# Gate and up of the dense feed-forward from chunk 1 on: weights stationary, tokens moving

## The chip, the cores and the metric

One core of one Trainium2 chip runs the whole program. The metric is the device time of one execution in microseconds (us); three runs are shown for the kernel before, and one execution was profiled.

## The reference, cut to what matters

Two stacks of two layers work on one sequence of S = 256 tokens of width D = 1024, in float32. Five feed-forwards among them are dense: one in the first stack's first layer, and two in each layer of the second stack. (The first stack's second layer has a mixture of eight experts instead.)

```python
def swiglu(x, wg, wu, wd):
    return (jax.nn.silu(x @ wg) * (x @ wu)) @ wd
...
def swiglu_2(x, w_gu, w_down):
    gate, up = jnp.split(x @ w_gu, 2, axis=-1)
    return (jax.nn.silu(gate) * up) @ w_down
...
        y = swiglu_2(rmsnorm(h, ffn1_pre_g[l]), ffn1_w_gu[l], ffn1_w_down[l])
        h = h + 0.5 * rmsnorm(y, ffn1_post_g[l])
```

The hidden width is 2816. In the second stack the input is normalised per token, and the result once more.

## The kernel before, in words

**Arithmetic.** Every float32 operand is split into a high part in the matmul's format and a low rest (`uT_hi`, `uT_lo` for the tokens, `hi_a`, `lo_a` for the gate/up weights, `hi_b` or `x_hi` and `lo_b` for the down weights, `hT_hi`, `hT_lo` for the hidden values). A product is three matmuls: high by high, low by high, high by low (`split3`, L660 to L662).

**Chunks.** A feed-forward goes over the hidden width in 11 chunks of 256 columns (`N_FCH`, `FCH`). For a chunk, `gate_up` (TensorE) multiplies the two token tiles of 128 (stationary: `uT`) by 512 moving columns, 256 of gate and 256 of up: 2 tiles x 8 slices of D x 3 products = 48 matmuls of 512 columns, into one PSUM bank per tile (`pp[:, 0]`, `pp[:, 1]`). ACT takes the silu of a tile's gate (`silu`, L1648), DVE multiplies it by the up half (`hidden`, L2286 or L2289), and the hidden values stand in `rows` with tokens on the partitions. The down product needs them the other way round: `turn` (L900) is four 128x128 transposes on TensorE into a bank of `tp`; ACT copies its high part (`hi_hidden`, L1656) and DVE the low one (`turned`, L2300). `down` is then 2 x 2 x 2 x 3 = 24 matmuls of 512 columns into `acc`.

**Order.** `ffn_walk` writes each engine's order: TensorE does `gate_up` of chunk c+1, then `down` of chunk c, then `turn` of chunk c+1. The turn of chunk 0 stands in the middle of `gate_up` of chunk 1, the turn of chunk 10 inside the down product of chunk 9. `gate_up` of a chunk waits on `s_ppv`, that is until DVE has made the chunk before's hidden values and so freed its banks, and on `s_alo` for its weights. ACT's and DVE's orders are fixed as well; in a chunk they hold, beside the steps above, the splitting of the weights two chunks ahead (L1642 and L2276, two halves each) and of the down weights (L1665 and L2313). On DVE a chunk's order is hidden of both tiles, first half of `lo_a`, `hT_lo`, `lo_b`, second half of `lo_a`.

**The per-token factor.** In the second stack `uT` is not yet normalised per token; ACT and DVE multiply by `pre_rstd` where a token is a partition (`scaled=True`: the silu's scale, and the scalar of L2286). POOL makes it in `pre_norm`, and the final normalisation's factor in `post_norm`.

Of the kernel before, what the change touches and what calls it, by code (L numbers as in the profile page):

```python
# [23 lines left out]
F32 = mybir.dt.float32  # L24
F32R = mybir.dt.float32r
# [7 lines left out]
P = 128  # L33
# [147 lines left out]
def program(nc, a, out):  # L181
    with ExitStack() as ctx:
# [29 lines left out]
        uT_hi = sb("uT_hi", [P, KD, S], F32R)  # L212
        uT_lo = sb("uT_lo", [P, KD, S], F32R)
# [44 lines left out]
        nlam = stat[:, 128:129]  # L258
        nsink = stat[:, 136:144]
# [14 lines left out]
        hi_c = x_hi[:, :, :].rearrange("p t d -> p (t d)")  # L274

# [54 lines left out]
        s_ppv = sem("s_ppv")  # L330
        s_acc = [sem("s_acc0"), sem("s_acc1")]
# [321 lines left out]
        def _(pe):  # L653
# [186 lines left out]
            def ffn(experts, sparse=False, ahead=False):  # L840

                a0, b0, g0, lo0, ppv0 = n["a"], n["b"], n["g"], n["lo"], n["ppv"]
                tiles = 1 if sparse else TT

# [24 lines left out]
                def gate_up(c, e, j):  # L869
# [6 lines left out]
                    if c.rest == 0:  # L876
                        wait_pp()
                    else:
                        pe.wait_ge(s_ppv, c.half * 4 + (2 * c.rest - opening + ppv0))
                    if sparse and isinstance(j, int) and j == 0:  # L880
                        pe.wait_ge(s_glo, e.index + 1)
                    wh = hi_a[:, slot, :].rearrange("p (g k n) -> p g k n", g=2, k=KD)
                    wl = lo_a[:, slot, :].rearrange("p (g k n) -> p g k n", g=2, k=KD)
                    for tt in range(tiles):
                        if opening and tt == 1:
                            turn(Chunk(c.half, c.rest - 1))
# [6 lines left out]
                def turn(c):  # L893
# [3 lines left out]
                    for kk in range(2):  # L897
                        for tt in range(tiles):
                            at = (kk * tiles + tt) * P
                            mm = nc.tensor.transpose(tp[:, bank, at:at + P],  # L900
# [34 lines left out]
                def side_b(c, e, j):  # L935
                    if not sparse and isinstance(j, int) and j == 0 and is_first(e):
                        pe.wait_ge(s_accfree, n["acc"])
                    if experts == 1 and isinstance(j, int) and j == N_FCH - 2:
                        enter(c)
                        part(c, 0, 0, e, j)  # L940
                        turn(c.next())
                        part(c, 0, 1, e, j)
                        part(c, 1, 0, e, j)
                        return
# [6 lines left out]
                    down(c, e, j).then_inc(s_bused, 1)  # L951
                    turn(c.next())
# [14 lines left out]
                def tail(c, e, j):  # L967
# [16 lines left out]
                    for tt in range(TT):  # L984
                        if experts == 1 and tt == 1:
                            part(Chunk(c.half, c.rest - 1), 1, 1, e, j - 1).then_inc(s_bused, 1)
                        for h in range(2):
                            part(c, 0, tt, e, j, (h,))
                            if ahead and tt == 1 and h == 1:
                                bank_free[0] = bank_free[1] = (s_tlo, lo0 + experts * N_FCH)  # L990
                                turn_ahead(g0 + experts * N_FCH, lo0 + experts * N_FCH)
# [6 lines left out]
                n["g"] += k  # L998
# [6 lines left out]
                pp_free[:] = [(s_ppv, n["ppv"] - 1), (s_ppv, n["ppv"])]  # L1005
# [123 lines left out]
            def mixer():  # L1129

                n["unit"] = 0
                fill_free[:] = pp_free
# [390 lines left out]
            for l in range(N_LAYERS):  # L1523
# [3 lines left out]
                ffn(1, ahead=True)  # L1527
# [3 lines left out]
                ffn(1, ahead=l + 1 < N_LAYERS)  # L1531
# [3 lines left out]
        def _(act):  # L1535
# [90 lines left out]
            def ffn(experts, final=False, sparse=False, scaled=False):  # L1626
                a1, b0, g0, pp0, bu0 = n["a"], n["b"], n["g"], n["pp"], n["bu"]
                tiles = 1 if sparse else TT
                last = experts * N_FCH - 1
# [14 lines left out]

                def silu(c, which=range(tiles)):
                    for tt in which:
                        act.wait_ge(s_pp, c.half * 4 + (2 * c.rest + tt + 1 + TT - tiles + pp0))
# [4 lines left out]
                def hi_hidden(c):  # L1652
                    slot = (b0 - 1 + c.rest) % 2
                    act.wait_ge(s_tps, c.at(g0 + 1))
                    ks = slice(slot, slot + 1) if sparse else slice(2 * slot, 2 * slot + 2)
                    nc.scalar.activation(hT_hi[:, ks, :].rearrange("p k s -> p (k s)"),  # L1656
                                         tp[:, (g0 + c.rest) % 2, 0:tiles * S], ACT.Copy).then_inc(s_thi, 1)
# [29 lines left out]
                def body(c, e, j):  # L1687
# [19 lines left out]
                    else:  # L1707
                        silu(c)
                        hi_next(c, 0)
# [24 lines left out]
                n["g"] += k  # L1734
                n["pp"] += 2 * k

# [388 lines left out]
        def _(dve):  # L2125
# [132 lines left out]
            def ffn(experts, final=False, sparse=False, scaled=False):  # L2258
                a1, b0, g0, hi0, ppa0, half0 = n["a"], n["b"], n["g"], n["thi"], n["ppa"], n["half"]
                bu0 = n["bu"] + 2  # L2260
                tiles = 1 if sparse else TT
                left = []

# [16 lines left out]

                def hidden(c, e, which=range(tiles)):
                    for tt in which:
                        dve.wait_ge(s_ppa, c.half * 4 + (2 * c.rest + tt + 1 + TT - tiles + ppa0))
                        o, s, u = rows[:, tt, FCH:2 * FCH], rows[:, tt, 0:FCH], pp[:, tt, FCH:2 * FCH]
                        if scaled:
                            ins = nc.vector.scalar_tensor_tensor(out=o, in0=s, scalar=pre_rstd[:, tt:tt + 1], in1=u,  # L2286
# [1118 lines left out]
```

## Time and profile before

| | |
|---|---|
| median of 3 runs | 2534.42 us (2533.99 to 2536.29) |
| span of the profiled execution | 2530.3 us |
| mean granted TensorE clock | 0.997 |
| PE busy | 98% of the span |
| weight loads (PEld) | 81% |
| DVE, ACT, POOL busy | 70%, 55%, 10% |

The span goes from the first to the last instruction. The profiled execution's own time is not listed; the runs shown lie 3.7 to 6.0 us above its span. Matmuls are pipelined: the duration of one (389 ns for 512 columns) is longer than the distance between two starts, and it is the distance between starts that adds up.

### The profile page before, as it was taken

How to read it: one execution, taken by the hardware profiler on the slowest of the kernel's cores; microseconds unless marked ns; L12 is line 12 of the kernel's file. 1: busy time of each engine (PE TensorE's matmuls, PEld its weight loads, DVE VectorE, ACT ScalarE, POOL GpSimd, SP SyncE). 2: the span in 40 equal slices, each digit the busy share in tenths (PEclk: the TensorE clock that was granted, in tenths of full speed). 3: DMA queues.
4: the chain of work that ended last, by engine and by line, in shares of the span. 5: the costliest groups of instructions: out<-in, count | busy, mean ns of one | idle time of the engine just before them, and what ended most of it. 6: DMA issues, size and time to landing. Idle time of an engine off the chain costs nothing.

```text
span 2530.3 us, 32402 instructions
## 1 busy us (share of the span) xinstructions
PE 2481.9 (98%) x11877; PEld 2036.9 (81%) x11877; DVE 1770.7 (70%) x1750; ACT 1395.4 (55%) x1524; POOL 248.4 (10%) x317
## 2 busy tenths in 40 slices
PE   9999999999999999999999999999999999999998
PEld 7778877878888888887788888878888888887887
DVE  5755557789989989999755667785555556778554
ACT  5543444677777777777644555454444445554533
POOL 3000021000000000000141103010004210300000
PEclk9999999999999999999999999999999999999999
DMA  7354444699999999999785343355548644435551
GB/s 274 142 224 175 174 137 172 259 360 366 368 364 358 371 361 363 368 368 353 264 263 212 135 190 142 135 208 208 190 160 253 220 153 172 166 142 199 196 187 67
DMA packets 89577, 595.83 MB, mean 235 GB/s; under 512 B 11616, under 2 KB 11760, under 8 KB 22016
## 3 DMA queue, kind: packets, MB, share of 16 engines
q1 hardware_dynamic: 77760, 558.99, 58.2%
q0 software_dynamic: 11712, 35.43, 5.1%
q8 instruction: 67, 1.10, 0.2%
q14 instruction: 38, 0.31, 0.0%
HBM read 588.09 MB, written 6.29 MB: 235 GB/s over the span
## 4 chain that ended last, share of the span: by engine, by line
PE 80%; DVE 9%; ACT 4%; issue 3%; DMA 3%; POOL 1%; SPq 0%; DVEq 0%; ACTq 0%; POOLq 0%
PE pp L660 17%; PE pp L662 17%; PE pp L661 17%; PE acc L660 7%; PE acc L662 7%; PE acc L661 7%; DVE lo_a L2797 2%; PE tp L900 2%; DMA raw_a<-in_moe_gu 1%; ACT hi_a L1581 1%; DVE lo_a L2185 1%; PE tp L672 1%; PE acc L1040 1%; PE tp L1089 1%; DVE lo_b L2313 1%
## 5 line engine op out<-in xcount | busy, mean ns | idle before, releaser
L660 PE MATMUL pp<-hi_a,uT_hi 128*128 128x512 f32 (+1 forms) x2140 | 852.5, 398 | 10.1 <-DVE uT_lo L2660 2.7
L662 PE MATMUL pp<-hi_a,uT_lo 128*128 128x512 f32 (+1 forms) x2140 | 832.4, 389 | 0.0
L661 PE MATMUL pp<-lo_a,uT_hi 128*128 128x512 f32 (+1 forms) x2140 | 830.4, 388 | 0.0
L2276 DVE TENSOR_TENSOR lo_a<-raw_a,hi_a 128x2048 fp32r<-128x2048 f32 x282 | 649.7, 2304 | 125.6 <-ACT hi_a L1642 124.7
L1642 ACT ACTIVATE hi_a<-raw_a 128x2048 fp32r<-128x2048 f32 x282 | 537.9, 1909 | 23.7 <-DMA raw_a<-in_moe_gu 23.2
L660 PEld LDWEIGHTS pp<-hi_a,uT_hi 128*128 128x128 f32 x2140 | 402.1, 188 | 92.0 <-issue 9.9
L662 PEld LDWEIGHTS pp<-hi_a,uT_lo 128*128 128x128 f32 x2140 | 401.7, 188 | 85.7
L661 PEld LDWEIGHTS pp<-lo_a,uT_hi 128*128 128x128 f32 x2140 | 402.8, 188 | 76.4
L661 PE MATMUL acc<-lo_b,hT_hi 128*128 128x512 f32 x792 | 308.2, 389 | 0.0
L2313 DVE TENSOR_TENSOR lo_b<-raw_b,hi_b 128x2048 fp32r<-128x2048 f32 x115 | 263.4, 2290 | 44.9 <-ACT hi_b L1665 44.0
L660 PE MATMUL acc<-hi_b,hT_hi 128*128 128x512 f32 x572 | 223.8, 391 | 2.8 <-DVE lo_b L2313 2.8
L662 PE MATMUL acc<-hi_b,hT_lo 128*128 128x512 f32 x572 | 223.0, 390 | 0.0
L1665 ACT ACTIVATE hi_b<-raw_b 128x2048 fp32r<-128x2048 f32 x115 | 220.0, 1913 | 4.0 <-DMA raw_b<-in_moe_wd 3.8
L1581 ACT ACTIVATE hi_a<-raw_a 128x2048 fp32r<-128x2048 f32 (+1 forms) x104 | 190.5, 1875 | 21.6 <-PE pp L662 13.9
L1656 ACT ACTIVATE hT_hi<-tp 128x256 fp32r<-128x256 f32 (+1 forms) x143 | 66.6, 466 | 243.2 <-PE tp L900 242.8
L661 PEld LDWEIGHTS acc<-lo_b,hT_hi 128*128 128x128 f32 x792 | 148.7, 188 | 30.3
L2797 DVE TENSOR_TENSOR lo_a<-raw_a,hi_a 128x2048 fp32r<-128x2048 f32 (+1 forms) x64 | 143.0, 2269 | 41.4 <-ACT hi_a L1581 39.8
L1648 ACT ACTIVATE rows<-pp,stat 128x256 f32<-128x256 f32 x88 | 41.8, 475 | 233.6 <-PE pp L662 230.7
L2300 DVE TENSOR_TENSOR hT_lo<-tp,hT_hi 128x256 fp32r<-128x256 f32 (+1 forms) x143 | 74.7, 523 | 111.3 <-ACT hT_hi L1656 111.3
L1648 ACT ACTIVATE rows<-pp 128x256 f32<-128x256 f32 x110 | 42.3, 385 | 186.6 <-PE pp L662 183.3
L2286 DVE SCALAR_TENSOR_TENSOR rows<-rows,stat,pp 128x256 f32<-128x256 f32 x88 | 41.6, 476 | 133.2 <-ACT rows L1648 133.2
L660 PEld LDWEIGHTS acc<-hi_b,hT_hi 128*128 128x128 f32 x572 | 107.4, 188 | 28.3 <-issue 3.9
(303 smaller groups left out, 2744.0 us busy)
## 6 DMA issues: line engine op xcount, KB each, us to landing
raw_a<-in_moe_gu SPq DMA_DIRECT2D x176, 1024.0 KB, 6.6
raw_a<-in_ffn_w_gu SPq DMA_DIRECT2D x88, 1024.0 KB, 6.7
raw_b<-in_moe_wd SPq DMA_DIRECT2D x87, 1024.0 KB, 8.5
raw_a<-in_w_in SPq DMA_DIRECT2D x70, 1024.0 KB, 6.8
raw_b<-in_ffn_w_down SPq DMA_DIRECT2D x44, 1024.0 KB, 4.9
raw_a<-in_ffn_gu SPq DMA_DIRECT2D x22, 1024.0 KB, 6.6
raw_a<-in_w_out SPq DMA_DIRECT2D x16, 1024.0 KB, 5.9
raw_a<-in_w_branch SPq DMA_DIRECT2D x12, 1024.0 KB, 6.0
```

The source lines that it names most:

```text
L660: nc.tensor.matmul(out_ap, l_hi, r_hi, start=start, stop=False, skip_group_check=True)
L661: nc.tensor.matmul(out_ap, l_hi, r_lo, start=False, stop=False, skip_group_check=True)
L662: return nc.tensor.matmul(out_ap, l_lo, r_hi, start=False, stop=stop, skip_group_check=True)
L1581: nc.scalar.activation(hi_a[:, slot, cs], raw_a[:, slot, cs], ACT.Copy) \
L1642: nc.scalar.activation(hi_a[:, slot, cs], raw_a[:, slot, cs], ACT.Copy) \
L1648: nc.scalar.activation(rows[:, tt, 0:FCH], pp[:, tt, 0:FCH], ACT.Silu, scale=pre_rstd[:, tt:tt + 1] if scaled else 1.0) \
L1656: nc.scalar.activation(hT_hi[:, ks, :].rearrange("p k s -> p (k s)"), tp[:, (g0 + c.rest) % 2, 0:tiles * S], ACT.Copy).then_inc(s_thi, 1)
L1665: nc.scalar.activation(dst[:, :], raw_b[:, slot, :] if src is None else src, ACT.Copy) \
L2276: ins = nc.vector.tensor_tensor(lo_a[:, slot, cs], raw_a[:, slot, cs], hi_a[:, slot, cs].bitcast(F32), ALU.subtract)
L2300: nc.vector.tensor_tensor(hT_lo[:, ks, :].rearrange("p k s -> p (k s)"), tp[:, (g0 + c.rest) % 2, 0:tiles * S], hT_hi[:, ks, :].rearrange( ...
L2313: nc.vector.tensor_tensor(lo_b[:, slot, :], src, hb[:, :].bitcast(F32), ALU.subtract).then_inc(s_blo, 1)
L2797: ins = nc.vector.tensor_tensor(lo_a[:, slot, cs], raw_a[:, slot, cs], hi_a[:, slot, cs].bitcast(F32), ALU.subtract)
```

## The change

From chunk 1 on, the weights are the stationary operand and all 256 tokens move. A chunk has two blocks of 128 hidden columns; for each, gate and up get a bank of their own: `tp[:, 0]`, `tp[:, 1]` for block 0 and `pp[:, 1]`, `pp[:, 0]` for block 1 (`block_bank`). Into a bank go, for each of the 8 slices of D, one matmul of 512 columns (high weights by high and low tokens side by side, which is why `uT` is now one tensor) and one of 256 (low weights by high tokens). That is 2 x 2 x 8 x 2 = 64 matmuls, 32 of each width. The bank then holds two halves that must still be added. The result has hidden columns on the partitions, as `down` needs it, so there is no turn for these chunks.

ACT copies the half with the low tokens to `rows` (`low_part`), DVE adds it to the other half (`block_sums`), for gate and for up; silu runs from `rows`, and `hT_hi` and `hT_lo` are made from `rows`. Chunk 0 stays as it was, with its turn, now into `pp[:, 0]`.

In the second stack a token is now a column, so DVE multiplies the gate's sum by a full tile `by_token` (one more operation per block); two transposes on TensorE (`turn_factors`) and an ACT copy (`factors`) make it at the start of chunk 1. The up half is left without the factor, and `post_norm` makes up for it with a scaled epsilon (`post_eps`).

```diff
+                def turn_factors():
...
+                    pe.wait_ge(s_pre, n["pre"])
+                    for tt in range(TT):
+                        mm = nc.tensor.transpose(pp[:, 0, tt * P:(tt + 1) * P],
+                                                 pre_rstd[:, tt:tt + 1].to_broadcast([P, P]), ident[:, :])
+                    mm.then_inc(s_tps, 1)
...
+                    for block in range(2):
+                        if opening and block == 1:
+                            if scaled:
+                                pe.wait_ge(s_bytoken, n["bytoken"])
+                            turn(Chunk(0, 0))
+                        ws = slice(block * P, (block + 1) * P)
+                        for g in range(2):
+                            if opening and block and g:
+                                pe.wait_ge(s_tlo, lo0 + 1)
+                            bank = block_bank(block, g)
+                            for k in range(KD):
+                                nc.tensor.matmul(bank.rearrange("p (c s) -> p c s", c=2), wh[:, g, k, ws], uT[:, :, k, :],
+                                                 start=(k == 0), stop=False, skip_group_check=True)
+                                mm = nc.tensor.matmul(bank[:, 0:S], wl[:, g, k, ws], uT_hi[:, k, :], start=False,
+                                                      stop=(k == KD - 1), skip_group_check=True)
+                            mm.then_inc((s_gate, s_pp)[g], 1)
...
+                    if dense and not (isinstance(j, int) and j == 0):
+                        if opening and scaled:
+                            turn_factors()
+                        gate_up_blocks(slot, opening)
+                        return
...
                     if experts == 1 and isinstance(j, int) and j == N_FCH - 2:
                         enter(c)
-                        part(c, 0, 0, e, j)
-                        turn(c.next())
-                        part(c, 0, 1, e, j)
-                        part(c, 1, 0, e, j)
+                        for kk, tt in ((0, 0), (0, 1), (1, 0)):
+                            part(c, kk, tt, e, j)
                         return
...
                     down(c, e, j).then_inc(s_bused, 1)
+                    if dense:
+                        return
                     turn(c.next())
...
                     for tt in which:
+                        if dense and not is_opening(c):
+                            low_part(c, tt, 0)
+                            act.wait_ge(s_gsum, c.half * 4 + (2 * c.rest + tt - 1 + gate0))
+                            nc.scalar.activation(rows[:, tt, 0:FCH], rows[:, tt, 0:FCH], ACT.Silu).then_inc(s_ppa, 1)
+                            low_part(c, tt, 1)
+                            continue
...
+                    if dense and not is_opening(c):
+                        act.wait_ge(s_ppv, c.half * 4 + (2 * c.rest + 2 + pp0))
+                        nc.scalar.activation(hT_hi[:, 2 * slot:2 * slot + 2, :], rows[:, :, FCH:2 * FCH], ACT.Copy) \
+                          .then_inc(s_thi, 1)
+                        return
...
+                    dve.wait_ge(s_low, c.half * 8 + (4 * c.rest + 2 * block - 3 + low0))
+                    ins = nc.vector.tensor_tensor(gate, block_bank(block, 0)[:, 0:S], low_gate, ALU.add)
+                    if scaled:
+                        ins.then_inc(s_graw, 1)
...
+                        ins = nc.vector.tensor_tensor(gate, gate, by_token, ALU.mult)
+                    ins.then_inc(s_gsum, 1)
+                    dve.wait_ge(s_low, c.half * 8 + (4 * c.rest + 2 * block - 2 + low0))
+                    nc.vector.tensor_tensor(low_up, block_bank(block, 1)[:, 0:S], low_up, ALU.add).then_inc(s_upsum, 1)
+                    dve.wait_ge(s_upsum, c.half * 4 + (2 * c.rest + block - 1 + low0 // 2))
+                    dve.wait_ge(s_ppa, c.half * 4 + (2 * c.rest + block + 1 + ppa0))
+                    nc.vector.tensor_tensor(rows[:, block, FCH:2 * FCH], gate, low_up, ALU.mult).then_inc(s_ppv, 1)
```

On TensorE, where a down product ends and the next `gate_up` begins (second stack, first feed-forward, chunk 1 to chunk 2), there stood before:

```order
L661 MATMUL acc<-lo_b,hT_hi 128x512
L662 MATMUL acc<-hi_b,hT_lo 128x512
L900 MATMUL tp<-ident,rows 128x128 [waits s_tlo,s_ppv]
L900 MATMUL tp<-ident,rows 128x128 x3
L660 MATMUL pp<-hi_a,uT_hi 128x512 [waits s_ppv,s_alo]
L661 MATMUL pp<-lo_a,uT_hi 128x512
L662 MATMUL pp<-hi_a,uT_lo 128x512
```

And now (lines are those of the changed kernel):

```order
L675 MATMUL acc<-lo_b,hT_hi 128x512
L676 MATMUL acc<-x_hi,hT_lo 128x512
L889 MATMUL tp<-uT,hi_a 128x512 [waits s_ppv,s_alo]
L891 MATMUL tp<-uT,lo_a 128x256
L889 MATMUL tp<-uT,hi_a 128x512
L891 MATMUL tp<-uT,lo_a 128x256
```

The four transposes are gone; the wait on `s_ppv` now stands at the first matmul of `gate_up` alone, and matmuls of two widths alternate.

On DVE, from the hidden values of chunk 0 to those of chunk 1 in the same feed-forward, there stood before:

```order
L2286 SCALAR_TENSOR_TENSOR rows<-rows,stat,pp 128x256 [waits s_ppa,s_pre]
L2286 SCALAR_TENSOR_TENSOR rows<-rows,stat,pp 128x256 [waits s_ppa]
L2276 TENSOR_TENSOR lo_a<-raw_a,hi_a 128x2048 [waits s_ahalf]
L2300 TENSOR_TENSOR hT_lo<-tp,hT_hi 128x512 [waits s_thi]
L2313 TENSOR_TENSOR lo_b<-raw_b,x_hi 128x2048 [waits s_bhi]
L2276 TENSOR_TENSOR lo_a<-raw_a,hi_a 128x2048 [waits s_ahi]
L2286 SCALAR_TENSOR_TENSOR rows<-rows,stat,pp 128x256 [waits s_ppa] x2
```

And now:

```order
L2376 TENSOR_TENSOR lo_a<-raw_a,hi_a 128x2048 [waits s_ahi]
L2386 TENSOR_TENSOR rows<-tp,rows 128x256 [waits s_low]
L2392 TENSOR_TENSOR rows<-rows,qkT 128x256 [waits s_graw,s_bytoken]
L2395 TENSOR_TENSOR rows<-tp,rows 128x256 [waits s_low]
L2398 TENSOR_TENSOR rows<-rows 128x256 [waits s_ppa,s_upsum]
L2386 TENSOR_TENSOR rows<-pp,rows 128x256 [waits s_low]
L2392 TENSOR_TENSOR rows<-rows,qkT 128x256 [waits s_graw]
L2395 TENSOR_TENSOR rows<-pp,rows 128x256 [waits s_low]
L2398 TENSOR_TENSOR rows<-rows 128x256 [waits s_ppa,s_upsum]
```

Behind the same second half of `lo_a`, two operations have become eight, with waits on ACT between them (`s_low` for the copies, `s_ppa` for the silu). `qkT` is where `by_token` lies; in the first stack L2392 is missing.

## Rows read from the trace of the kernel before

**Rows 1.** The page's first part: busy us, share of the span, instructions

```profile
PE 2481.9 (98%) x11877; PEld 2036.9 (81%) x11877; DVE 1770.7 (70%) x1750; ACT 1395.4 (55%) x1524; POOL 248.4 (10%) x317
```

**Rows 2.** Windows: one stretch in each dense feed-forward; columns in its first row

```profile
core 0: us, PE busy (x) PEld busy (x) DVE busy (x) ACT busy (x) POOL busy (x), PEclk, DMA share, GB/s
147.00:316.00 169.00, 168.88 (x766) 139.47 (x765) 88.99 (x71) 73.22 (x65) 0.79 (x2) 1.00 0.51 188
1264.00:1432.00 168.00, 168.00 (x763) 139.00 (x762) 93.10 (x66) 74.98 (x67) 39.75 (x50) 1.00 0.64 219
...
sum 839.00, PE 838.88 PEld 693.83 DVE 443.73 ACT 366.05 POOL 80.61; mean PE 167.78 PEld 138.77 DVE 88.75 ACT 73.21 POOL 16.12
```

**Rows 3.** Timeline of PE around one turn: start, duration, line, tile, count

```profile
1292.20 0.39 PE L662 MATMUL acc<-hi_b,hT_lo 128*128 128x512 f32 x1
1292.43 0.60 PE L900 MATMUL tp<-ident,rows 128*128 128x128 f32 x4
1292.78 0.48 PE L660 MATMUL pp<-hi_a,uT_hi 128*128 128x512 f32 x1
1293.10 0.40 PE L661 MATMUL pp<-lo_a,uT_hi 128*128 128x512 f32 x1
...
1294.03 0.39 PE L662 MATMUL pp<-hi_a,uT_lo 128*128 128x512 f32 x1
```

**Rows 4.** Timeline of PE: first turn, and the turns before and after

```profile
1264.26 0.60 PE L900 MATMUL tp<-ident,rows 128*128 128x128 f32 x4
...
1275.63 0.60 PE L900 MATMUL tp<-ident,rows 128*128 128x128 f32 x4
...
1309.24 0.60 PE L900 MATMUL tp<-ident,rows 128*128 128x128 f32 x4
```

**Rows 5.** Timeline of PE far from any turn

```profile
1300.17 0.39 PE L662 MATMUL pp<-hi_a,uT_lo 128*128 128x512 f32 x1
1300.40 0.39 PE L660 MATMUL pp<-hi_a,uT_hi 128*128 128x512 f32 x1
...
1303.57 0.39 PE L662 MATMUL pp<-hi_a,uT_lo 128*128 128x512 f32 x1
```

**Rows 6.** Timeline of PE and PEld in the mixer's 256-wide projection

```profile
1475.50 0.28 PE L662 MATMUL pp<-hi_a,uT_lo 128*128 128x256 f32 x1
1475.62 0.28 PE L660 MATMUL pp<-hi_a,uT_hi 128*128 128x256 f32 x1
...
1478.02 0.28 PE L662 MATMUL pp<-hi_a,uT_lo 128*128 128x256 f32 x1
...
1475.39 0.19 PEld L662 LDWEIGHTS pp<-hi_a,uT_lo 128*128 128x128 f32 x1
1475.51 0.19 PEld L660 LDWEIGHTS pp<-hi_a,uT_hi 128*128 128x128 f32 x1
```

**Rows 7.** Groups of instructions by line and form: count, busy us, mean ns

```profile
L662 PEld LDWEIGHTS pp<-hi_a,uT_lo 128*128 128x128 f32 x2140 | 401.7, 188 | 85.7
L2289 DVE TENSOR_TENSOR rows<-rows,pp 128x256 f32<-128x256 f32 x110 | 45.4, 413 | 37.0 <-ACT rows L1648 37.0
L2768 DVE TENSOR_TENSOR t<-mixb,rope 128x256 f32<-128x256 f32 x8 | 3.0, 418 | 0.1
L1648 ACT ACTIVATE rows<-pp 128x256 f32<-128x256 f32 x110 | 42.3, 385 | 186.6 <-PE pp L662 183.3 <-PE pp L865 3.2
L1656 ACT ACTIVATE hT_hi<-tp 128x512 fp32r<-128x512 f32 x55 | 32.9, 599 | 192.6 <-PE tp L900 192.6
```

**Rows 8.** Timeline of ACT and DVE from the first turn on (idle before, releaser)

```profile
1264.90 0.60 ACT L1656 ACTIVATE hT_hi<-tp 128x512 fp32r<-128x512 f32 x1 [4.34 <-PE tp L900]
1265.39 1.91 ACT L1665 ACTIVATE x_hi<-raw_b 128x2048 fp32r<-128x2048 f32 x1
1267.20 1.91 ACT L1642 ACTIVATE hi_a<-raw_a 128x2048 fp32r<-128x2048 f32 x1
1269.00 0.46 ACT L1648 ACTIVATE rows<-pp,stat 128x256 f32<-128x256 f32 x1
...
1265.53 0.69 DVE L2300 TENSOR_TENSOR hT_lo<-tp,hT_hi 128x512 fp32r<-128x512 f32 x1 [2.65 <-ACT hT_hi L1656]
1267.34 2.29 DVE L2313 TENSOR_TENSOR lo_b<-raw_b,x_hi 128x2048 fp32r<-128x2048 f32 x1 [1.12 <-ACT x_hi L1665]
1269.54 2.28 DVE L2276 TENSOR_TENSOR lo_a<-raw_a,hi_a 128x2048 fp32r<-128x2048 f32 x1
1271.75 0.86 DVE L2286 SCALAR_TENSOR_TENSOR rows<-rows,stat,pp 128x256 f32<-128x256 f32 x2
```

More of the change, by code:

```diff
@@ L274, in program, with block_bank @@
         hi_c = x_hi[:, :, :].rearrange("p t d -> p (t d)")
+        by_token = qkT[:, 0, 0:S]
+        def block_bank(block, g):
+            return (pp[:, 1 - g, :] if block else tp[:, g, :])
         def centred(tt):
@@ L1004, in ffn @@
                     bank_free[0] = bank_free[1] = (s_tlo, n["lo"])
-                pp_free[:] = [(s_ppv, n["ppv"] - 1), (s_ppv, n["ppv"])]
+                pp_free[:] = [(s_ppv, n["ppv"] - (not dense)), (s_ppv, n["ppv"])]
                 n["acc"] += 1
@@ L1628, in ffn @@
                 tiles = 1 if sparse else TT
+                dense, gate0 = experts == 1, n["gate"]
+                turns = 1 + scaled if dense else experts * N_FCH
                 last = experts * N_FCH - 1
@@ L1708, in body @@
                         silu(c)
+                        if scaled and is_opening(c):
+                            factors()
                         hi_next(c, 0)
@@ L2259, in ffn, with is_opening @@
                 a1, b0, g0, hi0, ppa0, half0 = n["a"], n["b"], n["g"], n["thi"], n["ppa"], n["half"]
+                low0, graw0 = n["low"], n["graw"]
                 bu0 = n["bu"] + 2
                 tiles = 1 if sparse else TT
+                dense = experts == 1
+                turns = 1 + scaled if dense else experts * N_FCH
                 left = []
+                if scaled:
+                    n["bytoken"] += 1
+                def is_opening(c):
+                    return isinstance(c.half, int) and c.at(0) == 0
                 def rest():
@@ L2298, in turned @@
                     dve.wait_ge(s_thi, c.at(hi0 + 1))
+                    if dense and not is_opening(c):
+                        ks = slice(2 * slot, 2 * slot + 2)
+                        nc.vector.tensor_tensor(hT_lo[:, ks, :], rows[:, :, FCH:2 * FCH], hT_hi[:, ks, :].bitcast(F32),
+                                                ALU.subtract).then_inc(s_tlo, 1)
+                        return
                     ks = slice(slot, slot + 1) if sparse else slice(2 * slot, 2 * slot + 2)
                     nc.vector.tensor_tensor(hT_lo[:, ks, :].rearrange("p k s -> p (k s)"),
-                                            tp[:, (g0 + c.rest) % 2, 0:tiles * S],
+                                            (pp[:, 0, :] if dense else tp[:, (g0 + c.rest) % 2, :])[:, 0:tiles * S],
                                             hT_hi[:, ks, :].rearrange("p k s -> p (k s)").bitcast(F32),
@@ L2377, in ffn @@
                 n["bu"] += k - 1
-                n["g"] += k
+                n["g"] += turns
+                if dense:
+                    n["low"] += 4 * (k - 1)
+                if scaled:
+                    n["graw"] += 2 * (k - 1)
                 n["thi"] += k
```

87 lines of the change are left out of this document (62 added, 25 removed).

## The prediction

> **What bounds the kernel now.** The page first: PE is busy for 98% of the span, weight loads for 81%, DVE for 70% and ACT for 55% [rows 1]. That is an average, so the stretches in which the change acts are read next: in one window in each dense feed-forward PE is busy 838.88 of 839.00 us, at a granted clock of 1.00 (the 2.4 GHz level), while DVE has 443.73 and ACT 366.05 us of work in them [rows 2]. In these stretches no other engine ends a wait, and the time is the sum of what TensorE issues. That sum is read from starts, not from durations. Far from a turn, 512-wide matmuls start every (1303.57 - 1300.17) / 15 = 0.2267 us [rows 5]. A chunk has 48 + 24 = 72 of them, 16.32 us. From turn to turn it takes (1309.24 - 1275.63) / 2 = 16.805 us [rows 4]. The difference, 0.485 us, is the price of a turn, and the timeline shows where it lies: the four transposes start at 1292.43, just where the next matmul would have, and the sixth matmul of `gate_up` starts at 1294.03, not at 1292.43 + 5 x 0.2267 = 1293.56 [rows 3].
>
> **What the change removes.** Of 11 turns in a feed-forward the one of chunk 0 stays. 10 x 5 = 50 turns go: 50 x 0.485 = -24.3 us.
>
> **What it adds on TensorE.** The columns stay the same (32 x 768 = 48 x 512), but 48 matmuls become 64, and each has its own start. The nearest row for a 256-wide one is the mixer's 256-wide projection: they start every (1478.02 - 1475.50) / 21 = 0.120 us [rows 6]. A chunk's `gate_up` is then 32 x (0.2267 + 0.120) = 11.09 us in place of 48 x 0.2267 = 10.88: +0.213, in 50 chunks +10.7 us. No row shows the two widths in turn. The bound below is half a wide one, 0.113 (nothing added); the bound above is the slow rival below. I take the sum of the two rows, because in either stretch the distance is the columns' time plus about 13 ns, so nothing but the columns sets it.
>
> What speaks against 256-wide matmuls is the weight load: one shows 188 ns [rows 7], longer than 120. But in that stretch the loads start 0.12 us apart and overlap [rows 6]. The Trainium skill ("TensorE: Matmul & The Clock Gate", Back-to-back issue gap) gives a warm distance of N/2.4 + 2.5 ns, 215.8 and 109.2; by it the added cost would be 0.042 us a chunk and the forecast 8.6 us lower, but the trace differs by 11 ns at either width, and the sum goes by the trace.
>
> In the four scaled feed-forwards `turn_factors` adds two transposes: by the turn's price less two starts of 0.11 us (within a turn, (1292.78 - 1292.43) / 4 = 0.09 to 0.485 / 4 = 0.12 each [rows 3]) 0.27 us each, in all +1.1 us. What they wait for (`s_pre`, the first tile's hidden values) is what the first silu and this `gate_up` waited for before.
>
> **What it adds on ACT and DVE, and what hides it.** Per block: ACT two copies and a silu of 256 columns, 0.385 us each by the silu's row; DVE two sums from PSUM, 0.413, and one or two products in SBUF, 0.418 [rows 7]. A scaled chunk has some 3.3 us of such DVE work in place of 0.95: ten chunks add some 24 us to some 90 in a window of 168 [rows 2]. As work it is covered; what counts is a wait that comes too late.
>
> In steady state that is `s_ppv`, before the next `gate_up`. Behind the last up matmul stand: ACT copy 0.39, DVE sum 0.41, product 0.42, with hops of about 0.04 (the copy ends at 1265.50, DVE starts at 1265.53 [rows 8]): some 1.35 us. `down` of the chunk before covers 24 x 0.2267 = 5.44. Cost nothing; without that cover it would be the 1.35.
>
> At the end, `down` of chunk 10 waits for `s_tlo`: those 1.35, then the ACT copy 0.60 and DVE's rest 0.69 [rows 7, 8], some 2.7 us, behind 18 matmuls of chunk 9, 4.08 us. Nothing again, with 1.4 us to spare. Before, the turn sat between.
>
> At the opening it is different. From the first turn ACT does `hT_hi`, the down weights' high part and half of `hi_a`, up to 1269.0; DVE follows with `hT_lo`, `lo_b` and half of `lo_a`, and comes to chunk 1's hidden values at 1271.75, 7.49 us behind the turn's start [rows 8]. Both tiles then took 0.86. TensorE wanted them at 1275.63, 11.37 behind [rows 4]; now, with 16 pairs in place of 24 wide matmuls in between (+0.11), at 11.48. So 4.0 us are there. In them DVE has two blocks to do, and each is a chain: sum 0.41, times `by_token` 0.42, silu and copy on ACT 0.68 (the second starts about 0.09 before the first ends), sum 0.41, product 0.42, four hops 0.16: 2.5 us. The second block's data are long there, but DVE and ACT take the blocks in order, so two blocks are 5.0 us. TensorE stands for 1.0 us before `gate_up` of chunk 2. In the unscaled feed-forward a block is 2.04 and two are 4.1: 0.1. In all 4 x 1.0 + 0.1 = +4.1 us. Bounds: nothing, if operations overlap more; 2 us each, if a hop costs 0.15. Late next is chunk 1's own splitting and so chunk 2's hidden values; there DVE has another 11 + 5.4 us, and nothing more is lost.
>
> The larger `ss` work on POOL is one operation on two columns behind `s_pre`, beside TensorE's matmuls; no DMA is added or moved.
>
> **Sum.** -24.3 + 10.7 + 1.1 + 4.1 = -8.4 us on a span of 2530.3. The median lies 4.1 above that span, by what no row shows and the change doesn't touch: 2534.4 - 8.4 = 2526.0 us.
>
> **Rivals.**
> - *Weight loads bind, and it becomes slower.* With 88 loads of 188 ns a chunk has 16.5 us of them in about 16.5 us. If a narrow matmul between wide ones can't hide the next load, a pair costs two loads, 376 ns, not 347: 32 x 50 x 0.029 = +47 us, 2573 us. It decides from a pair of 352 ns on, since 1600 x 5.3 ns eat the 8.4 us. The overlapping loads speak against it [rows 6]; for it, that no row has the two widths mixed. The Trainium skill ("Perfetto Trace Analysis", Identifying the Most-Contended Engine) would judge TensorE by the busy share of loads, which by its rule would leave no room here; the 256-wide stretch, where loads fill more than the time, does not bear that out as a bound.
> - *A wait in every chunk.* If the ping-pong between ACT and DVE ends later than 5.44 us behind the last matmul, each chunk loses; 0.17 us a chunk make it no faster, 0.5 make it 2542 us. The chain has 4 us to spare.
> - *No stall at the opening.* The chains overlap better than I add them: 2526.0 - 4.1 = 2521.9 us.
> - *Twice the stall at the opening, or one at the end too.* Some 1 us more at 4 or 5 places: 2530 to 2531 us, the same as far as can be told.
> - *The change does nothing*, because the turn's time was a wait's in disguise: against it, PE's busy 838.88 of 839.
>
> **How the numbers follow.** About 0.2%, 5 us, is what a measurement of this kernel can tell from no change. The forecast as summed (2522.5 to 2529) has 0.55, no stall at the opening 0.16: faster 0.71. More stall, or nothing gained, 0.14: same. Loads that bind 0.09, waits in every chunk or at other places 0.06: slower 0.15. The range goes from a stall of nothing with a slightly dearer turn, 2520.5, to 2532.5, where a doubled stall meets pairs a few ns dearer; it leaves the slow cases and a part of the case without change outside.
>
> **What the profile afterwards would show.** `gate_up` at 11.09 us and a chunk at 16.53 from one first matmul to the next, with starts 0.227 and 0.120 us apart in turn; any pair above 0.35 makes the second term wrong. One turn in each dense feed-forward. Idle time of PE before the first matmul of `gate_up` of chunk 2, put down to DVE's product at L2398, about 1 us in four feed-forwards and near nothing in the first; idle there in other chunks makes the covers wrong. No idle before the down product of chunk 10. DVE some 100 us busier in all.

## The result, and the profile after

The changed kernel takes 2546.1 us in the median, the kernel before, timed beside it, 2537.8: a ratio of 1.0031 (1.0017 to 1.0046), slower by 8 us where the prediction said 8 us faster. Timed again on another occasion the ratio was 1.0034 (1.0020 to 1.0048). The profiled execution has a span of 2544.3 us, 14.0 above the one that the sum was made against. Three executions that were disturbed as a whole (4103 us of the changed kernel, 11290 and 2603 us of two experiments) are left out of everything.

The page's first part of the changed kernel, to be held against [rows 1]:

```profile
PE 2485.5 (98%) x12485; PEld 2059.2 (81%) x12485; DVE 1885.7 (74%) x2030; ACT 1461.9 (57%) x1728; POOL 252.4 (10%) x321
```

DVE is 115 us busier, some 100 were forecast, and ACT 66. TensorE has 608 matmuls more and is still busy for 98%: what made the kernel slower must again be read from starts, in two places.

**The chunk.** The timeline of PE in the middle of a `gate_up` of the changed kernel (start, duration, line, tile):

```profile
1355.94 0.40 PE L889 MATMUL tp<-uT,hi_a 128*128 128x512 f32 x1
1356.17 0.28 PE L891 MATMUL tp<-uT,lo_a 128*128 128x256 f32 x1
1356.29 0.40 PE L889 MATMUL tp<-uT,hi_a 128*128 128x512 f32 x1
1356.53 0.28 PE L891 MATMUL tp<-uT,lo_a 128*128 128x256 f32 x1
...
1360.18 0.40 PE L889 MATMUL pp<-uT,hi_a 128*128 128x512 f32 x1
```

Twelve pairs take 4.24 us, 0.3535 each, not 0.3467. The narrow matmul costs 0.117, no more than among its own kind; it is the wide one that takes some 0.236 where it took 0.2267 among wide ones [rows 5]. And the starts of two down products six chunks apart, with the `gate_up` that follows the first, in the same view:

```profile
1315.45 0.40 PE L674 MATMUL acc<-x_hi,hT_hi 128*128 128x512 f32 x1
...
1320.96 0.39 PE L889 MATMUL tp<-uT,hi_a 128*128 128x512 f32 x1
...
1416.21 0.40 PE L674 MATMUL acc<-x_hi,hT_hi 128*128 128x512 f32 x1
```

A chunk takes 100.76 / 6 = 16.793 us. Its down product takes 1320.96 - 1315.45 = 5.51 of them, the rest, 11.28, is `gate_up`; forecast were 5.44 and 11.09. Before, a chunk took 16.805 [rows 4]. The turn is gone, and nothing came of it.

**The opening.** The waits of PE over the span (us in all, times, longest), and the starts of the first two down products of the first scaled feed-forward:

```profile
PE tp L889 <- DVE rows L2398: 4.8, 4, 1.8
```

```profile
1278.51 0.40 PE L674 MATMUL acc<-x_hi,hT_hi 128*128 128x512 f32 x1
...
1298.71 0.40 PE L674 MATMUL acc<-hi_b,hT_hi 128*128 128x512 f32 x1
```

Four waits of 1.84, 1.04, 0.94 and 1.04 us before `gate_up` of chunk 2, where they were expected and put down to the product that was named, with 1.0 each forecast. But in the feed-forward with the 1.84 this chunk takes 20.20 us, 3.4 more than the others. The windows there (columns as in [rows 2]) and the timeline show what lies behind the wait:

```profile
1284.00:1286.00 2.00, 0.16 (x2) 0.06 (x1) 1.04 (x3) 1.78 (x3) 0.14 (x1) 1.00 1.13 373
1286.00:1288.00 2.00, 2.00 (x7) 1.77 (x8) 1.26 (x1) 2.00 (x3) 0.00 (x0) 0.58 0.86 242
1288.00:1290.00 2.00, 2.00 (x8) 1.66 (x8) 2.00 (x3) 2.00 (x2) 0.00 (x0) 0.57 1.02 422
1290.00:1292.00 2.00, 2.00 (x13) 1.75 (x12) 2.00 (x2) 1.10 (x2) 1.29 (x3) 1.00 0.55 225
```

```profile
1285.97 0.47 PE L889 MATMUL tp<-uT,hi_a 128*128 128x512 f32 x1 [1.84 <-DVE rows L2398]
...
1286.45 0.63 PE L889 MATMUL tp<-uT,hi_a 128*128 128x512 f32 x1
1286.88 0.41 PE L891 MATMUL tp<-uT,lo_a 128*128 128x256 f32 x1
1287.09 0.63 PE L889 MATMUL tp<-uT,hi_a 128*128 128x512 f32 x1
```

TensorE had stood idle for 1.84 us; then the granted clock is 0.58 and 0.57 in two windows (most of each at 1.2 GHz), a pair takes 0.64 us, and at 1290 the clock is back at 1.00. Nearly half of that chunk's loss is this, not the wait.

**The stages that weren't changed.** Up to the last down product the two profiles differ by 14.0 us. 7.4 of them lie between the end of the first feed-forward and the end of the mixture of experts, and only 6.6 in all the rest: 918.3 us before, 925.7 after. More on that below.

### The profile page after: what moved, and what is told of

Its sections match the earlier page's. It is cut to its first block, busy times and chain, and to the rows that moved or that the text cites. A ratio compares the mean times of both kernels' runs of the same rounds, so it can differ in the third digit from the quotient of the medians.

```text
span 2544.3 us, 34318 instructions
## 1 busy us (share of the span) xinstructions
PE 2485.5 (98%) x12485; PEld 2059.2 (81%) x12485; DVE 1885.7 (74%) x2030; ACT 1461.9 (57%) x1728; POOL 252.4 (10%) x321
## 4 chain that ended last, share of the span: by engine, by line
PE 75%; DVE 10%; DMA 5%; ACT 5%; issue 4%; POOL 1%; SPq 0%; DVEq 0%; ACTq 0%; POOLq 0%
PE pp L674 9%; PE pp L676 9%; PE pp L675 9%; PE tp L889 7%; PE pp L889 7%; PE acc L674 6%; PE acc L676 6%; PE acc L675 6%; PE tp L891 4%; PE pp L891 3%; DMA raw_b<-in_moe_wd 3%; DVE lo_a L2925 2%; DMA raw_a<-in_moe_gu 1%; DVE lo_a L2376 1%; ACT hi_a L1635 1%
## 5 line engine op out<-in xcount | busy, mean ns | idle before, releaser
L674 PE MATMUL pp<-hi_a,uT 128*128 128x512 f32 (+1 forms) x1340 | 536.7, 400 | 6.1 <-ACT rows L2059 2.3
L676 PE MATMUL pp<-hi_a,uT 128*128 128x512 f32 (+1 forms) x1340 | 521.3, 389 | 0.0
L675 PE MATMUL pp<-lo_a,uT 128*128 128x512 f32 (+1 forms) x1340 | 519.7, 388 | 0.0
L674 PEld LDWEIGHTS pp<-hi_a,uT 128*128 128x128 f32 x1340 | 252.4, 188 | 56.5 <-issue 8.2
L676 PEld LDWEIGHTS pp<-hi_a,uT 128*128 128x128 f32 x1340 | 252.0, 188 | 53.8
L889 PE MATMUL tp<-uT,hi_a 128*128 128x512 f32 x800 | 286.3, 400 | 5.5 <-DVE rows L2398 4.8
L675 PEld LDWEIGHTS pp<-lo_a,uT 128*128 128x128 f32 x1340 | 252.8, 189 | 46.7
L889 PE MATMUL pp<-uT,hi_a 128*128 128x512 f32 x800 | 284.8, 399 | 0.0
L2437 DVE TENSOR_TENSOR lo_b<-raw_b,hi_b 128x2048 fp32r<-128x2048 f32 x115 | 263.2, 2289 | 20.5 <-ACT hi_b L1752 20.1
L891 PE MATMUL tp<-uT,lo_a 128*128 128x256 f32 x800 | 225.3, 282 | 0.0
L891 PE MATMUL pp<-uT,lo_a 128*128 128x256 f32 x800 | 224.6, 281 | 0.0
L889 PEld LDWEIGHTS tp<-uT,hi_a 128*128 128x128 f32 x800 | 151.1, 189 | 44.0 <-issue 6.8
L889 PEld LDWEIGHTS pp<-uT,hi_a 128*128 128x128 f32 x800 | 150.3, 188 | 36.9
```

The lines of the kernel that those rows point to most:

```text
L674: nc.tensor.matmul(out_ap, l_hi, r_hi, start=start, stop=False, skip_group_check=True)
L675: nc.tensor.matmul(out_ap, l_hi, r_lo, start=False, stop=False, skip_group_check=True)
L676: return nc.tensor.matmul(out_ap, l_lo, r_hi, start=False, stop=stop, skip_group_check=True)
L889: nc.tensor.matmul(bank.rearrange("p (c s) -> p c s", c=2), wh[:, g, k, ws], uT[:, :, k, :], start=(k == 0), stop=False, skip_group_check= ...
L891: mm = nc.tensor.matmul(bank[:, 0:S], wl[:, g, k, ws], uT_hi[:, k, :], start=False, stop=(k == KD - 1), skip_group_check=True)
L2437: nc.vector.tensor_tensor(lo_b[:, slot, :], src, hb[:, :].bitcast(F32), ALU.subtract).then_inc(s_blo, 1)
```

## The experiments

**The turn alone.** The kernel before, with the transposes of chunks 1 to 10 left out in the dense feed-forwards:

```diff
                 pe.wait_ge(s_tlo, c.at(lo0 - 1))
+                if experts == 1 and c.rest + (0 if isinstance(c.half, int) else 2) > 0:
+                    pe.sem_inc(s_tps, 1)
+                    return
                 for kk in range(2):
```

> The kernel before with the transposes of chunks 1 to 10 left out in its dense feed-forwards (their results are then not those of the reference: the hidden values' turned form is stale); the waits stay. It measures the first term alone: if a turn costs what was read, 0.485 us, a chunk is 16.32 us and the kernel 24 us faster than the kernel before, some 2513. If something else paces a chunk at 16.79, which is what both kernels take, it stays there and nothing is gained.

It took 2509.6 us, ratio 0.9894 (0.9877 to 0.9910): 27 us less, between 23 and 31. Its rows come from a second run:

> The kernel before without the transposes of chunks 1 to 10 once more, for its rows: a chunk of 72 wide matmuls at 16.32 us if the price of a turn is 0.485, between 16.32 and 16.80 if part of the price was the widths' change or a wait.

2510.3 us, and in the timeline the starts of down products six chunks apart:

```profile
1299.94 0.39 PE L660 MATMUL acc<-x_hi,hT_hi 128*128 128x512 f32 x1
...
1397.86 0.39 PE L660 MATMUL acc<-x_hi,hT_hi 128*128 128x512 f32 x1
```

97.92 / 6 = 16.320 us, to the last digit what 72 wide matmuls were said to take. The price of a turn was right, and nothing else paces a chunk at 16.79: that both kernels take nearly the same is chance.

**The pair by itself.** The changed kernel with some 570 matmuls behind its last one, while the other engines run out of work (`wide_rows` moves 512 columns of weights, `wide_blocks` both parts of the tokens as L889 does, `narrow` is as L891):

```diff
...
+            for wide_one in (wide_rows, wide_blocks):
+                for i in range(48):
+                    wide_one(i % KD)
+                for i in range(48):
+                    wide_one(i % KD)
+                    narrow(i % KD)
+                for run in (2, 8):
+                    for i in range(48 // run):
+                        for k in range(run):
+                            wide_one(k)
+                        for k in range(run):
+                            narrow(k)
...
```

> The changed kernel with some 570 matmuls behind its last one, on operands that are left there (no output depends on them), while the other engines finish and then stand idle: 48 wide ones in a row, 48 pairs, runs of two and two and of eight and eight, first with a wide matmul whose moving operand is one piece (weights), then with the two-piece one (high and low part of the tokens), then 64 narrow ones. If the change of width is what costs: wide in a row 227 ns for both kinds, pairs 354 for both, runs of eight some 348 per pair. If the two-piece operand costs: 227 in a row for one kind and 236 for the other. If ACT's and DVE's work beside it costs: pairs at 347 here, where nothing runs beside them. In time some 130 us longer.

The timeline of PE: the one-piece kind in a row and in pairs, then its runs of two, then two starts of runs of eight (a row with x2 or x49 is a group, and begins at its first start), then the two-piece kind:

```profile
2536.50 11.27 PE L1593 MATMUL tp<-hi_a,uT 128*128 128x512 f32 x49
2547.60 0.28 PE L1597 MATMUL pp<-uT,lo_a 128*128 128x256 f32 x1
2547.72 0.40 PE L1593 MATMUL tp<-hi_a,uT 128*128 128x512 f32 x1
...
2562.09 0.28 PE L1597 MATMUL pp<-uT,lo_a 128*128 128x256 f32 x1
...
2565.02 0.63 PE L1593 MATMUL tp<-hi_a,uT 128*128 128x512 f32 x2
2565.49 0.39 PE L1597 MATMUL pp<-uT,lo_a 128*128 128x256 f32 x2
2565.72 0.63 PE L1593 MATMUL tp<-hi_a,uT 128*128 128x512 f32 x2
2566.18 0.40 PE L1597 MATMUL pp<-uT,lo_a 128*128 128x256 f32 x2
2566.41 0.40 PE L1593 MATMUL tp<-hi_a,uT 128*128 128x512 f32 x1
...
2583.82 0.40 PE L1593 MATMUL tp<-hi_a,uT 128*128 128x512 f32 x1
...
2586.61 0.40 PE L1593 MATMUL tp<-hi_a,uT 128*128 128x512 f32 x1
...
2597.79 11.30 PE L1589 MATMUL tp<-uT,hi_a 128*128 128x512 f32 x49
2608.92 0.28 PE L1597 MATMUL pp<-uT,lo_a 128*128 128x256 f32 x1
...
2610.69 0.28 PE L1597 MATMUL pp<-uT,lo_a 128*128 128x256 f32 x1
```

In a row a wide one takes (2547.60 - 2536.50) / 49 = 0.2265, the two-piece kind 0.2271. In pairs it is (2562.09 - 2547.60) / 41 = 0.3534 and (2610.69 - 2608.92) / 5 = 0.354. So it is neither the operand in two pieces nor the work of ACT and DVE, which stood still from 2544 on: it is the alternation. Runs of two bring four wide and four narrow ones to 1.39 us, 0.348 a pair; runs of eight take 2.79 / 8 = 0.349. Neither is the sum of the two rows, 0.3465, but both lie much nearer to it than the pairs in turn.

**The order in the kernel.** First eight and eight within each bank:

```diff
                             for k in range(KD):
                                 nc.tensor.matmul(bank.rearrange("p (c s) -> p c s", c=2), wh[:, g, k, ws], uT[:, :, k, :],
                                                  start=(k == 0), stop=False, skip_group_check=True)
+                            for k in range(KD):
                                 mm = nc.tensor.matmul(bank[:, 0:S], wl[:, g, k, ws], uT_hi[:, k, :], start=False,
```

> Order within a bank changed: the eight 512-wide matmuls first, then the eight 256-wide ones, in place of pairs. If it is the change of width that makes a wide matmul dear (236 ns behind a narrow one in the changed kernel, 227 among its own kind) and only the first one behind a narrow one pays, gate_up is 32 x (0.2281 + 0.120) = 11.14 us in place of 11.32 and the kernel some 9 us faster than the changed one, some 2537. If the slowness dies out over seven to ten matmuls, as the rows behind the turns of the kernel before show it, the wide ones still average some 232 ns, gate_up is some 11.26 and only 3 us come back. If wide matmuls are slow because their moving operand comes in two pieces (high and low part of the tokens), or because ACT and DVE read PSUM beside them, they stay at 236 in a row: gate_up 11.4, no gain.

2535.0 us, ratio 0.9997 (0.9985 to 1.0008) to the kernel before, some 9 us less than the changed kernel has by its ratios, as the first case of the expectation says. In the timeline, down products six chunks apart:

```profile
1314.26 0.40 PE L674 MATMUL acc<-x_hi,hT_hi 128*128 128x512 f32 x1
...
1413.94 0.40 PE L674 MATMUL acc<-x_hi,hT_hi 128*128 128x512 f32 x1
```

A chunk takes 99.68 / 6 = 16.613: 0.18 less, in 50 chunks 9 us, from the order of the same 64 matmuls. Then all 32 wide ones first:

```diff
                         for g in range(2):
                             if opening and block and g:
                                 pe.wait_ge(s_tlo, lo0 + 1)
...
+                            wide_part(block, g)
+                            if opening:
+                                narrow_part(block, g)
+                    if not opening:
+                        for block in range(2):
+                            for g in range(2):
+                                narrow_part(block, g)
```

> From chunk 2 on all 32 wide matmuls of gate_up first, then the 32 narrow ones, bank by bank; chunk 1 stays in pairs. Cost of changing widths: the narrow ones cost 32 x 0.120 = 3.84 us, the wide ones 32 x 0.227 = 7.26 plus some 0.06 for the slow first ones, gate_up 11.16 in place of 11.32 and, with some 0.06 in down behind the narrow ones as now, a chunk of 16.63: 45 x 0.16 = 7 us faster than the changed kernel, some 2539. Rival, two-piece operand or contention: wide ones at 236 in a row, gate_up 11.4, no gain. The gates come ready only in the last 3.8 us of gate_up, so the last hidden values end some 2 us behind it; down covers 5.4, and no new wait is expected.

Chunk 1 (`opening`) has eight wide and eight narrow ones a bank in this code, not the pairs that the expectation names. In the timeline, down products six chunks apart:

```profile
1313.38 0.40 PE L674 MATMUL acc<-x_hi,hT_hi 128*128 128x512 f32 x1
...
1412.70 0.40 PE L674 MATMUL acc<-x_hi,hT_hi 128*128 128x512 f32 x1
```

A chunk takes 99.32 / 6 = 16.553 us, even less than expected and within 0.02 of the prediction's 16.53: kept apart, the two widths cost what it added up. But the kernel takes 2555.7, ratio 1.0077 (1.0057 to 1.0098). The new wait that wasn't expected is there, five times, 14.9 us in all. In the first scaled feed-forward the waits of PE and the timelines of DVE and ACT read:

```profile
PE acc L674 <- DVE hT_lo L2432: 3.2, 1, 3.2
```

```profile
1429.09 0.43 DVE L2410 TENSOR_TENSOR rows<-rows 128x256 f32<-128x256 f32 x1
1430.43 2.29 DVE L2449 TENSOR_TENSOR lo_b<-raw_b,x_hi 128x2048 fp32r<-128x2048 f32 x1 [0.92 <-ACT x_hi L1764]
1432.64 0.42 DVE L2398 TENSOR_TENSOR rows<-pp,rows 128x256 f32<-128x256 f32 x1
...
1435.85 0.69 DVE L2432 TENSOR_TENSOR hT_lo<-rows,hT_hi 128x512 fp32r<-128x512 f32 x1 [0.69 <-ACT hT_hi L1744]
```

In chunk 10 alone the code puts the low part of the down weights (2.29 us on DVE, behind 1.90 on ACT) between the two blocks. With pairs, block 0 is through before; with the gates of all blocks coming at the end, the second block waits for it, and the down product for the second block. The expectation counted two blocks and left that step out.

**The opening.** Chunk 0's turn one bank earlier in `gate_up` of chunk 1:

```diff
                     for block in range(2):
-                        if opening and block == 1:
-                            if scaled:
-                                pe.wait_ge(s_bytoken, n["bytoken"])
-                            turn(Chunk(0, 0))
...
                         for g in range(2):
+                            if opening and not block and g:
+                                if scaled:
+                                    pe.wait_ge(s_bytoken, n["bytoken"])
+                                turn(Chunk(0, 0))
```

> The turn of chunk 0 stands before the first block's up part in chunk 1's gate_up, 2.8 us earlier than between its blocks. If the wait before gate_up of chunk 2 (1.84, 1.04, 0.94 and 1.04 us in the four scaled feed-forwards, some 0.1 in the other) comes from what ACT and DVE do behind that turn, it goes wholly: 4.9 us faster than the changed kernel, some 2541. Rival: chunk 0's hidden values and the copy of the factors are late for the earlier turn, and TensorE waits there, up to 0.5 us each; 3 us come back. Rival: the wait is set by DVE's two blocks alone: no change.

2534.1 us, ratio 0.9994 (0.9984 to 1.0004), by the ratios some 10 us less than the changed kernel. No wait of L889 for L2398 is left, and the first scaled feed-forward's down products of chunks 0 and 1 start, in the timeline:

```profile
1269.24 0.40 PE L674 MATMUL acc<-x_hi,hT_hi 128*128 128x512 f32 x1
...
1286.00 0.40 PE L674 MATMUL acc<-hi_b,hT_hi 128*128 128x512 f32 x1
```

16.76 us apart, in place of 20.20; in the other feed-forwards 16.74 to 16.76 in place of 18.04, 17.94, 17.84 and 16.96. That is 3.4 + 1.3 + 1.2 + 1.1 + 0.2 = 7.2 us for waits of 4.9 us. The other two profiles of the changed kernel, read in the same way, lose 7.0 us for 5.0 us of waits, with a fallen clock, and 5.1 us for 4.6, with the clock at 1.00 throughout. The timed runs show some 3 us more than 7.2; in the profiles the mixture of experts is 3 to 4 us shorter as well, see below.

**Both.** Wide first in chunks 2 to 9, bank by bank in chunks 1 and 10, the turn early:

```diff
-                        gate_up_blocks(slot, opening)
+                        gate_up_blocks(slot, opening, opening or isinstance(j, int) and j == N_FCH - 1)
```

> The changed kernel with the early turn of chunk 0, the wide matmuls first in chunks 2 to 9, and bank by bank (eight wide, eight narrow) in chunks 1 and 10, so that the last chunk's gates don't all come ready at the end. If the costs found so far add up: chunks 2 to 9 at 16.55 us and chunk 10 at 16.61, where the kernel before takes 16.80, no wait at the opening and none before the last down product: 40 x 0.25 + 10 x 0.19 = 12 us faster than the kernel before, some 2524, ratio 0.995. If the gain of the order and that of the early turn overlap or a new wait comes at the end (up to 3 us in each feed-forward): 2530 to 2536.

2528.2 us, ratio 0.9970 (0.9959 to 0.9982): faster than both kernels. In its timeline:

```profile
1305.60 0.40 PE L674 MATMUL acc<-x_hi,hT_hi 128*128 128x512 f32 x1
...
1404.92 0.40 PE L674 MATMUL acc<-x_hi,hT_hi 128*128 128x512 f32 x1
```

99.32 / 6 = 16.553 us a chunk, and neither wait in any of the five. Without the stretch from the first feed-forward's end to the end of the mixture of experts, the time to the last down product is 1594.4 us, 10.6 to 12.9 less than in three profiles of the kernel before; the median shows 7.5 of it.

**The stages that weren't changed.** The changed kernel again, timed, then both kernels side by side on one chip:

> The changed kernel once more, beside the kernel before. The dense feed-forwards' own rows make it some 6.5 us slower (ratio 1.0026); the other 7 us of difference between the two profiles lie in the mixture of experts, whose code is the same. If that stage varies from run to run, the ratio is 1.0015 to 1.0035 and the stage takes some other time in this profile, between 917 and 926 us; if the change slows that stage too, it is 1.004 or more and the stage takes 925 again.

> The kernel before once more, for the stages that the change doesn't touch. So far the mixture of experts took 778 to 782 us in two profiles of kernels with the old dense feed-forward and 784 to 786 in three of the changed one. If the stage only varies from run to run, it falls anywhere from 777 to 788 here; if the change slows it, it is 782 or less again.

> The changed kernel, on the same chip as the two looks at the kernel before. If the mixture of experts only varies from run to run, it takes 777 to 788 us; if the change slows it, 784 or more once more.

> As the other look at the kernel before: 777 to 788 us in the mixture of experts if it only varies, 782 or less if the changed kernel alone is slow there.

From the first matmul that gathers tokens for an expert (L822, in the changed kernel L836) to the last down product of the mixture of experts, the three profiles of the kernel before have 778.3, 778.2 and 781.6 us, the one without turns 782.2; the changed kernel has 784.8, 783.8 and 783.6, and 786.1 with the added matmuls behind it. With eight and eight the stage takes 788.5, and wide first 786.3. ACT's waits for that stage's weights in two profiles from one chip, first `before_b`, then `after_c`:

```profile
ACT hi_a L1642 <- DMA raw_a<-in_moe_gu: 17.9, 22, 2.4
```

```profile
ACT hi_a L1698 <- DMA raw_a<-in_moe_gu: 30.7, 29, 2.8
```

The weights come later there. The other two profiles of the kernel before have 23.2 and 26.0 us of these waits, of the changed kernel 32.0 and 31.3. With the early turn in all five feed-forwards the stage took 780.5 and, with the wide ones first as well ("Both"), 781.8 us, so the turn was moved in the scaled feed-forwards alone (g1, below) and in the unscaled one alone (g2, with `not scaled`):

```diff
-                        if opening and block == 1:
+                        if opening and block == 1 and not (scaled):
...
+                            if opening and not block and g and scaled:
```

> The early turn in the four scaled feed-forwards alone, which all run after the mixture of experts. Dense rows: some 7 us faster than the changed kernel. If the expert stage's 4 us follow from what runs ahead of it, they stay (784 us or more there, 31 us of waits for its gate-up weights), and the kernel is some 2538; if they follow from how the program as a whole lies, or from chance, the stage can take 778 to 782.

> The early turn in the unscaled feed-forward alone, the one that runs ahead of the mixture of experts. Dense rows: 0.2 us faster than the changed kernel. If the expert stage's lateness comes from that feed-forward's opening, the stage takes 780 to 782 us with some 20 us of waits and the kernel is some 4 us faster than the changed one; if not, 784 or more and no change.

> The early turn in all five once more, for the expert stage alone: 780 to 782 us with some 20 us of waits for gate-up weights if that was no chance; 784 or more if it was.

The profiles have 791.7 us (42.5 of waits) in g1, 784.3 (31.8) in g2 and 780.8 (23.4) in the repeat. By these g1 is the worst of all, but its profiled execution is the slowest of its ten (2545.9; they go down to 2533.5), and its median is 2538.0, ratio 1.0012 (0.9999 to 1.0025), by the ratios some 5 us under the changed kernel's where its dense rows ask for 7. g2 has 1.0019 (1.0000 to 1.0038), too wide to tell whether anything was gained. All eight profiles of the new feed-forwards without the early turn in all five lie above 783.5 us in this stage, the other seven profiles at or below 782.2. But up to the end of this stage g2 does the same work in the same order as the kernel with the early turn, and takes 784.3 where that took 780.5 and 780.8, so what runs ahead of the stage doesn't explain it by itself. Single profiles of one kernel differ by 3.4 us in this stage, and by some 4 in the mixer ahead of it (136.4 and 140.0 us in two of the kernel before): the longer one has a granted clock of 0.5 from 442 to 452 us, the other 1.00. Whether the changed kernel is really some 3 us slower there, and by what, stays open.

## Why the prediction was wrong, by its own steps

**What bounds the kernel, and the turn's price.** Right: 0.485 us read, 16.805 - 16.320 measured, 50 x 0.485 = -24.3, and 23 to 31 us in the timed runs.

**The 16 added matmuls.** This is the step that failed: "the sum of the two rows, because in either stretch the distance is the columns' time plus about 13 ns, so nothing but the columns sets it". Both rows were of stretches of one width. In turn a pair takes 0.3535, and `gate_up` 11.28 in place of 10.88, +0.40. The down product behind it takes 5.51 in place of 5.44, a term that the prediction didn't have. Together a chunk pays 16.793 - 16.320 = 0.473 for the added matmuls, not 0.213. In 50 chunks that is +23.7 us in place of +10.7, and nearly the whole gain of the turns. The prediction named the pair's price from which the sign turns, 352 ns, and gave it 9 in 100. The price came, 353.5 ns, but not by that rival's reason: two loads one behind the other would be 376 ns, and in runs of two the same loads cost 348 a pair. The runs show that the mixture costs more than its parts; why it does stays open. The Trainium skill's warm gap of a single matmul ("TensorE: Matmul & The Clock Gate", Back-to-back issue gap) errs on the same side: an estimate by it is 215.8 + 109.2 = 325 ns a pair.

**The factors.** Right, small. Timeline of PE at the third scaled opening:

```profile
1910.40 0.38 PE L869 MATMUL pp<-ident,stat 128*128 128x128 f32 x2
1910.54 0.48 PE L889 MATMUL tp<-uT,hi_a 128*128 128x512 f32 x1
1910.97 0.40 PE L889 MATMUL tp<-uT,hi_a 128*128 128x512 f32 x1
```

The second pair starts 0.57 us behind the first transpose, where one pair takes 0.35: 0.22 each, 0.9 in all, forecast 1.1. Three of the four stand idle for 0.4 us before them; in the kernel before, three of the same `gate_up` stood idle for 0.5.

**Work on ACT and DVE, and its covers.** Right: no wait in the steady chunks, none at the end. The cover at the end was what the wide-first order used up.

**The opening.** Mechanism and place right, price too low. The timeline of DVE in the second scaled feed-forward has a block as it was added up, from its first sum to the next block's, 2.5 us forecast:

```profile
1737.06 0.42 DVE L2386 TENSOR_TENSOR rows<-pp,rows 128x256 f32<-128x256 f32 x1
1737.51 0.43 DVE L2392 TENSOR_TENSOR rows<-rows,qkT 128x256 f32<-128x256 f32 x1
1738.69 0.43 DVE L2395 TENSOR_TENSOR rows<-pp,rows 128x256 f32<-128x256 f32 x1 [0.76 <-ACT rows L1712]
1739.15 0.42 DVE L2398 TENSOR_TENSOR rows<-rows 128x256 f32<-128x256 f32 x1
```

1739.57 - 1737.06 = 2.51. Three of four waits are within 0.06 us of the forecast. In the first scaled feed-forward one product of the other block took 1.33 us instead of 0.42, and that is the wait's 1.84 in place of 0.94. The timelines of POOL and DVE there:

```profile
1281.80 1.30 POOL L3338 TENSOR_TENSOR bias<-bias,mask 128x512 f32<-128x512 f32 x1
1282.06 1.33 DVE L2398 TENSOR_TENSOR rows<-rows 128x256 f32<-128x256 f32 x1
```

The product began inside an addition of POOL and ended 0.29 us behind it. In ten of the eleven profiles with the new feed-forwards a product of DVE, with both operands in SBUF, meets this addition; it ends 0.29 to 0.30 us behind it each time, wherever it began, and takes 1.00 to 2.09 us. A sum with an operand in PSUM that began inside the addition (eight and eight) took its usual 0.42. By that regular end it is POOL's addition that held DVE's product up, though no run leaves the addition out. The prediction reckoned with POOL's work behind `s_pre` alone. The sum also left out that a wait of TensorE costs more than its length: 7.2 us for 4.9 in this profile, most of the rest by the fallen clock, and 5.1 for 4.6 in the profile whose clock stayed at 1.00.

**Sum.** -24.3 + 23.7 + 0.9 + 7.2 = +7.5, against 6.6 between the two profiles outside the mixer and the experts; the 0.9 was not followed further. Of the 15.9 us between -8.4 and +7.5, 13.0 come from the added matmuls and 3.1 from the opening: with the added matmuls priced right, the opening alone would have made 2529. The medians show 8 to 9 us; the rest is what those unchanged stages vary by, or the open 3 us. The kernel before itself had 2537.8 us beside the changed one, 3.4 more than the 2534.4 of the sum; the ratio on 2534.4 is 2542, still far above the range. One side sum of the prediction is wrong: 0.5 us a chunk are 25 us, 2551 and not 2542; the forecast doesn't use it.

## What to carry to other kernels

A matmul's price read from a stretch of one shape holds for that shape in a row: where a change mixes widths, price the mixture, or keep each width in runs: eight and eight gave back 9 us by order alone. Where a small price stands 1600 times, 7 ns of error are more than the whole forecast. And when runs are regrouped, look for what the first and last chunk have that the others haven't: the same order that saved 0.24 us a chunk lost 3 us at each end.

## What the hardware showed unexpectedly

A 512-wide matmul behind a 256-wide one starts its successor after some 0.236 us, not 0.227, with the other engines idle and whichever operand moves; the cause isn't known. A product of DVE on SBUF that met an addition of POOL ended 0.29 us behind it, in ten profiles. The granted clock fell behind the opening's wait of 1.84 us and behind two of 2.0 in other runs (the chunk then took 20.2 to 20.5 us); behind four of 1.6 to 1.8 at the same place it stayed at 1.00, and the chunk lost about the wait. The Trainium skill ("TensorE: Matmul & The Clock Gate", HAM oscillation) describes idle gaps that cost more than themselves in this way; here they did so in three runs of seven.
